# The modulation's lane sums: from TensorE and ScalarE to GpSimd and DRAM

## The reference

```python
silu_c, silu_cc = jax.nn.silu(c), jax.nn.silu(c_ctx)           # 2048 numbers each
mod  = silu_c  @ w_mod[l] + b_mod[l]                           # w_mod[l]: 2048 x 6144
shift, scale, gate = jnp.split(mod[:, None, :], 3, axis=-1)
cmod = silu_cc @ w_mod[l] + b_mod[l]
cshift, cscale, cgate = jnp.split(cmod, 3)
h  = rmsnorm(x,  norm_g[l]) * (1.0 + scale)  + shift           # l = 0, 1
hc = rmsnorm(cx, norm_g[l]) * (1.0 + cscale) + cshift
...
x = x + gate * (y @ w_o[l])
```

## Time and profile before

| | us |
|---|---|
| median of three runs | 2954.16 |
| lowest, highest | 2953.43, 2954.73 |
| profiled execution: span, first to last instruction | 2953.0 |
| its own time outside the span | none is given; the median lies 1.2 above the span |

### The profile page before, as it was taken

One profiled execution on the slowest core, in us unless ns is written; L12 is line 12 of the kernel. 1 busy time (PEld: TensorE's weight loads), 2 busy tenths in 40 slices (PEclk: granted clock), 3 DMA queues, 4 the chain that ended last, 5 costly groups with the idle time before them and its releaser, 6 DMA issues.

```text
span 2953.0 us, 37150 instructions
## 1 busy us (share of the span) xinstructions
PE 2917.4 (99%) x14067; PEld 2392.3 (81%) x14067; DVE 1942.1 (66%) x2730; ACT 1266.1 (43%) x2044; POOL 216.7 (7%) x303
## 2 busy tenths in 40 slices
PE   9999999999999999999999999999999999999998
PEld 7897788888888888888888887777888888878877
DVE  6886466668868888888865834445545645666655
ACT  5443355553444344443555223333333324435444
POOL 1000000011001001010100000000000100102000
PEclk9999999999999999999999999999999999999999
DMA  8987956568767878878764743333343653766444
GB/s 281 297 299 266 314 175 193 151 201 283 254 211 266 279 259 277 271 263 279 266 205 140 230 137 122 117 111 129 106 139 130 228 185 90 258 228 208 136 137 156
DMA packets 313557, 611.05 MB, mean 207 GB/s; under 512 B 29303, under 2 KB 90452, under 8 KB 312484
## 3 DMA queue, kind: packets, MB, share of 16 engines
q1 hardware_dynamic: 294236, 544.74, 57.0%
q0 software_dynamic: 18176, 62.61, 5.9%
q10 hardware_dynamic: 968, 1.33, 0.1%
HBM read 567.93 MB, written 41.84 MB: 206 GB/s over the span
## 4 chain that ended last, share of the span: by engine, by line
PE 94%; DVE 3%; ACT 1%; issue 1%; DMA 0%; POOL 0%; SPq 0%; POOLq 0%; ACTq 0%; DVEq 0%
PE acc L679 28%; PE acc L681 27%; PE acc L680 27%; PE acc L1491 3%; PE acc L1465 2%; PE acc L1479 2%; DVE w_lo L496 1%; PE acc L1042 1%; PE acc L1463 1%; ACT w_hi L490 1%; PE acc L1440 1%; PE acc L756 0%; PE acc L609 0%; PE acc L705 0%; DVE at_st L1654 0%
## 5 line engine op out<-in xcount | busy, mean ns | idle before, releaser
L679 PE MATMUL acc<-w_hi,a_hi 128*128 128x512 f32 (+3 forms) x3736 | 1482.8, 397 | 8.6 <-DVE w_lo L496 6.5
L681 PE MATMUL acc<-w_hi,a_lo 128*128 128x512 f32 (+3 forms) x3736 | 1447.8, 388 | 0.0
L680 PE MATMUL acc<-w_lo,a_hi 128*128 128x512 f32 (+3 forms) x3736 | 1445.0, 387 | 0.0
L496 DVE TENSOR_TENSOR w_lo<-raw,w_hi 128x1024 fp32r<-128x1024 f32 (+3 forms) x778 | 932.2, 1211 | 342.1 <-ACT w_hi L490 337.2
L490 ACT ACTIVATE w_hi<-raw 128x1024 fp32r<-128x1024 f32 (+3 forms) x778 | 805.4, 1047 | 723.2 <-PE acc L681 671.4
L679 PEld LDWEIGHTS acc<-w_hi,a_hi 128*128 128x128 f32 x3736 | 702.6, 188 | 165.5 <-issue 18.7
L681 PEld LDWEIGHTS acc<-w_hi,a_lo 128*128 128x128 f32 x3736 | 701.7, 188 | 142.8
L680 PEld LDWEIGHTS acc<-w_lo,a_hi 128*128 128x128 f32 x3736 | 703.3, 188 | 126.5
L533 DVE SCALAR_TENSOR_TENSOR lanes_b<-raw,ct,lanes_b 128x1024 f32<-128x1024 f32 x150 | 189.5, 1305 | 0.0
L533 DVE SCALAR_TENSOR_TENSOR lanes_c<-raw,ct,lanes_c 128x1024 f32<-128x1024 f32 x120 | 157.6, 1357 | 0.0
L1537 ACT ACTIVATE pb<-acc,at_st 128x256 f32<-128x256 f32 (+4 forms) x144 | 71.1, 494 | 137.7 <-DVE at_st L1652 90.2
(11 more groups left out here) (422 smaller groups left out, 1772.9 us busy)
## 6 DMA issues: line engine op xcount, KB each, us to landing
raw<-in_w_mod SPq DMA_DIRECT2D x192, 512.0 KB, 4.8
raw<-in_w_in SPq DMA_DIRECT2D x128, 512.0 KB, 5.1
raw<-in_w_mlp_in SPq DMA_DIRECT2D x128, 512.0 KB, 4.3
raw<-in_w_mlp_out SPq DMA_DIRECT2D x128, 512.0 KB, 5.4
raw<-in_e_w_in SPq DMA_DIRECT2D x104, 512.0 KB, 4.0
raw<-in_w_o SPq DMA_DIRECT2D x64, 512.0 KB, 5.6
raw<-in_o_w_in SPq DMA_DIRECT2D x64, 512.0 KB, 4.6
raw<-in_w_in SPq DMA_DIRECT2D x56, 448.0 KB, 5.0
```

The costliest lines, as they stand in the source:

```text
L496: nc.vector.tensor_tensor(w_lo[:, n % SPLITS, 0:size], raw[:, r % RAWS, 0:size], w_hi[:, n % SPLITS, 0:size].bitcast(F32), ALU.subtract)\
L679: nc.tensor.matmul(o, s.lhs(0, kt, tt), wh, start=kt == 0 and not s.goes_on, stop=False)
L680: nc.tensor.matmul(o, s.lhs(0, kt, tt), wl, start=False, stop=False)
L681: last = nc.tensor.matmul(o, s.lhs(1, kt, tt), wh, start=False, stop=end)
```

## The change

The four functions go. In their place stands one on GpSimd, `lanes_reduce`, tied to nine steps of the walk. It waits for the piece's adds, adds each of the lanes' four quarters (128 x 512) over the partitions in place (the sum then stands in every partition), waits for that, and takes partition 0 as the row of 2 x 1024. In pieces 4 and 5 it halves the row and stores its two halves to MODF. Then it stores the row to a new DRAM tensor MODR, waits until it has landed, loads it back into `mc` with 128 numbers down the partitions and eight columns per vector, element by element, waits again, and counts `lanes_out` up itself. The hook of a step runs behind that step's stores or squares.

```diff
@@ -24,6 +24,7 @@
 P = 128
 DM = 2048
 KT = DM // P
+NPIECE = 10
 SEQ = 256
 CTX = 256
 HD = 128
@@ -217,6 +218,7 @@
         CMPK = dram("CMPK", (HD, 2 * NCMP))
         CMPV = dram("CMPV", (2 * NCMP, HD))
         MODF = dram("MODF", (2, 2, DM))
+        MODR = dram("MODR", (NPIECE, 2, CH))
         U2 = dram("U2", (CTX + SEQ, 6656))
         O2 = dram("O2", (CTX + SEQ, DM))
         U3 = dram("U3", (CTX + SEQ, 4416))
@@ -445,7 +447,8 @@
         ct_ready, bias_in, bias_zero = sem("ct_ready"), sem("bias_in"), sem("bias_zero")
         vec_ctx, vec_x = sem("vec_ctx"), sem("vec_x")
         lanes_done, lanes_out = sem("lanes_done"), sem("lanes_out")
-        sums_done, sums_kept, sums_turned = sem("sums_done"), sem("sums_kept"), sem("sums_turned")
+        lanes_reduced, row_halved, row_out, row_back = (sem("lanes_reduced"), sem("row_halved"), sem("row_out"),
+                                                        sem("row_back"))
         WIDE = tuple(range(NQ - 1))
 
 
@@ -599,43 +602,28 @@
             if upto == 2 * CH // P:
                 last.then_inc(lanes_done, 1)
 
-        def lanes_sum(pe, j):
-
-            pe.wait_ge(vec_ctx, KT * (j + 1))
-            pe.wait_ge(vec_x, KT * (j + 1))
-            if j:
-                pe.wait_ge(lanes_out, j)
+        def lanes_reduce(pool, j):
+
+            pool.wait_ge(vec_ctx, KT * (j + 1))
+            pool.wait_ge(vec_x, KT * (j + 1))
             for q in range(4):
-                last = nc.tensor.matmul(acc[32 * q:32 * q + 32, 4, :], ones[:, 0:32],
-                                        lanes_of(j)[:, q // 2, q % 2 * G:(q % 2 + 1) * G], start=True, stop=True)
-            last.then_inc(sums_done, 1)
-
-        def sums_keep(act, j):
-
-            act.wait_ge(sums_done, WIDE.index(j) + 1)
-            gate = j in (4, 5)
-            nc.scalar.activation(lanes_of(j)[:, 0, 0:G], acc[:, 4, :], ACT.Copy, scale=0.5 if gate else 1.0)\
-              .then_inc(sums_kept, 1)
-            if gate:
-                act.wait_ge(sums_kept, WIDE.index(j) + 1)
+                t = lanes_of(j)[:, q // 2, q % 2 * G:(q % 2 + 1) * G]
+                nc.gpsimd.partition_all_reduce(t, t, P, bass.bass_isa.ReduceOp.add).then_inc(lanes_reduced, 1)
+            pool.wait_ge(lanes_reduced, 4 * (j + 1))
+            row = lanes_of(j)[0:1, :, :]
+            if j in (4, 5):
+                nc.gpsimd.tensor_scalar(row, row, 0.5, None, ALU.mult).then_inc(row_halved, 1)
+                pool.wait_ge(row_halved, j - 3)
                 for v in range(2):
-                    act.dma_start(MODF[0, v, (j - 4) * CH:(j - 3) * CH].rearrange("(h n) -> h n", h=2),
-                                  lanes_of(j)[64 * v:64 * v + 64:32, 0, 0:G]).then_inc(rows_put, 16)
-
-        def sums_turn(pe, j):
-
-            pe.wait_ge(sums_kept, WIDE.index(j) + 1)
-            for i in range(4):
-                last = nc.tensor.transpose(acc[:, 4, i * P:(i + 1) * P], lanes_of(j)[:, 0, i * P:(i + 1) * P], ident[:, :])
-            last.then_inc(sums_turned, 1)
-
-        def sums_out(act, j):
-
-            act.wait_ge(sums_turned, WIDE.index(j) + 1)
+                    pool.dma_start(MODF[0, v:v + 1, (j - 4) * CH:(j - 3) * CH], lanes_of(j)[0:1, v, :]).then_inc(rows_put, 16)
+            pool.dma_start(MODR[j:j + 1, :, :], row).then_inc(row_out, 16)
+            pool.wait_ge(row_out, 16 * (j + 1))
             layer, c = (0, 8 * j) if j < 6 else (1, 8 * (j - 6))
-            nc.scalar.activation(mc[:, layer, :, c:c + 8].rearrange("p v (h i) -> p v h i", h=2),
-                                 acc[:, 4, :].rearrange("p (i v h x) -> p v h i x", i=4, v=2, h=2)[:, :, :, :, 0], ACT.Copy)\
-              .then_inc(lanes_out, 1)
+            for v in range(2):
+                pool.dma_start(mc[:, layer, v, c:c + 8], MODR[j, v, :].rearrange("(n p) -> p n", p=P),
+                               allow_slow_non_contiguous=True).then_inc(row_back, 16)
+            pool.wait_ge(row_back, 32 * (j + 1))
+            pool.sem_inc(lanes_out, 1)
 
         def lanes_keep(act, j):
             act.wait_ge(lanes_done, 1)
@@ -647,10 +635,9 @@
         beside = {}
         for j, ((name, i, c), (name2, i2, c2)) in enumerate(zip(sum_spots, keep_spots)):
             if j in WIDE:
-                places, at, _ = sum_wide[j]
-                for n, engine, f in ((0, "pe", lanes_sum), (5, "act", sums_keep), (6, "pe", sums_turn), (11, "act", sums_out)):
-                    name, i, c = places[at + n]
-                    stages[name].hook(engine, i, c, lambda eng, f=f, j=j: f(eng, j))
+                name, i = (("qkv", 5), ("gates_a", 0), ("mlp", 1), ("mlp", 5), ("mlp", 11), ("mlp", 14), ("mlp", 19),
+                           ("mlp", 22), ("mlp", 27))[j]
+                stages[name].hook("pool", i, 0, lambda pool, j=j: lanes_reduce(pool, j))
                 continue
             places, at, wide = sum_wide[j]
             for m in range(wide):
```

## The result

| | before | after |
|---|---|---|
| median us (4 runs each, same chip) | 2954.44 | 2986.36 |
| lowest, highest | 2953.43, 2955.94 | 2981.26, 2987.61 |
| span of the profiled execution | 2953.0 | 2985.8 |
| granted clock of TensorE, mean | 0.999 | 0.994 |

After is slower: ratio 1.0105, 95% interval 1.0091 to 1.0120, 31.9 us. I had forecast +104 us.

The account below looks back on a forecast made before the run. TensorE, busy 99% of the span, was taken to bound the kernel. Losses of 116.5 us at GpSimd's places less 12.9 us saved gave +103.6 us, a span of 3056.6 and a median of 3058 us; range 2941 to 3600 us.

Parts of the forecast that it names:

- piece 2: Reduction ahead of MLP step 2's squares, which TensorE transposes: window 27.2 us, needed 65.6, lost 38.4.
- piece 8: Reduction ahead of the mid_gain and sub_row loads, for which VectorE waits: window 19.0 us, needed 60.6, lost 41.6.
- R: One GpSimd all-reduce over 128x512, four per piece: taken as eight passes, 11.4 us; bounds 1.15 to 103 us.
- the windows: At each of nine places, how long GpSimd may be away before TensorE stands; losses there summed to 116.5 us.
- rival 1: All hidden: R near a single pass and no load, so every window is wide enough; 2941 us, chance 0.13.
- contention, at nothing: Slowing of VectorE's adds beside GpSimd's all-reduces, put at 0 us in the forecast.
- The bound that I worked out for it: VectorE's adds slowed throughout a reduction: about 12 us for each of seven pieces, up to +84 us.
- The saving: Lane sum (0.99 us) and turning (0.44 us) gone from TensorE, nine times: 12.9 us.
- The load: GpSimd loading code at each change of kind, 14 times, 5 us each.
- The DRAM trip: The row to DRAM and back into columns, issued by GpSimd: 10 us per piece, between 5.5 and 13.3.
- The halving: Pieces 4 and 5 also halve the row on GpSimd, 2048 columns on one partition: about 1.9 us.
- Pieces 0, 1 and 4: Waits for the clearing of cmp_v, for q and behind the bias row: lost 3.4, 6.2 and 19.5 us.

Follow-up runs that it names:

- e5: The changed kernel without its 36 all-reduces; partition 0's partial sums still go through DRAM: 2941.02 us, ratio 0.9955 to the kernel before.
- e4: The changed kernel with each of the 36 all-reduces covering one column of its 128x512 tile: 2946.02 us, ratio 0.9964 to the kernel before.
- e3: The changed kernel with both moves, that of e1 and that of e2, together: 2962.51 us, ratio 1.0027 to the kernel before.
- e6: The kernel before plus three groups of 12 all-reduces (maximum, 128x512) on GpSimd in the MLP, where nobody waits for them: 2964.03 us, ratio 1.0030.
- e1: The changed kernel with piece 2's reduction moved to step 3 of the stage before the MLP: 2972.31 us, ratio 1.0059 to the kernel before.
- e2: The changed kernel with the loads of mid_gain and sub_row put ahead of piece 8's reduction: 2973.86 us, ratio 1.0068 to the kernel before.
- e8: The kernel before with its lane sums kept on TensorE, but the turning replaced by the row through DRAM on ScalarE's queue: 2951.04 us, ratio 0.9986.

## Why the prediction was wrong

**The balance, from the runs.** Off TensorE: 2941.02 - 2954.44 = -13.4 (e5). The loads: +5.0 (e4 over e5). The two narrow places: +23.9 (after over e3). The rest of the all-reduces' time, beside VectorE: +16.5 (e3 over e4). Sum +31.9, as measured. The last two terms are not sharp: e4 keeps the narrow places, so what they cost with hardly any all-reduce is in its 5.0. Against e5 the rest is 21.5 us, loads included. e6 bears the last term out from outside: 9.3 us for 71.3 us of all-reduces, so 16 us for the 123.7 us in after, or 25 us if it goes by what VectorE lost (21.4 us there, 57.5 in e3). The traces say the same by place. Against e5, matmul by matmul, after falls behind by 17.3 us at piece 2, by 9.6 at piece 8, and by 21.1 at the other seven, 48.0 in all.

**The step that failed first: R.** "Eight passes", 11.4 us, a count of halvings priced with a square. Measured: 3.4 us, inside my bounds and near their lower end. Everything that I lost at the windows was made of 4R = 45.6 where 13.7 was true. By the formula of my own rival 1 (the places lose 8R - 11.2) R = 3.44 gives +3 us, 2957 us. With the measured load and DRAM trip put in as well, the same windows give a loss of 14.1 us at piece 2 and 14.4 at piece 8, near the 14.1 and 12.5 that were measured: the windows hold, R didn't. The rival had the right condition; I should have seen that the forecast hung on a number for which no row spoke, and that its two ends gave opposite signs.

**The step that failed second: "contention, at nothing".** The row was before me: VectorE's adds at 4.04 us beside a square. I dismissed it because an all-reduce "touches memory far more thinly". The trace says that a split or add beside it isn't done before it is, 3.3 us in place of 1.2. e6 shows the same with no other change, and operations with a PSUM input stay clean. The bound that I worked out for it would have missed it too: with 4R = 13.8, VectorE's 12.0 us of work become 19.6 by the ratio 4.04 / 2.47 (which makes the prediction's 39.7 us 65, not 64), less 1.8 us of idle and 5.6 of cushion, that is nothing. The size of VectorE's part holds, though not as an even slowing: (1999.6 - 1942.1) / 9 = 6.4 us more per piece in e3, where the bound has 7.6. The cushion doesn't. Of 6.4 us, 1.8 to 2.4 reached the end (16.5 to 21.5 us over nine pieces), and in e6 3.1 of 7.1 a group: idle and buffers together take some 4 us, not 7.4.

**Point by point.** The saving: 12.9 predicted, 13.4 measured, right. The load: 5 us predicted, at a change of kind only, right in kind and in number; 6.0 to 9.3 measured. The DRAM trip: 10 us predicted, 13.6 measured (933.82 to where the columns have landed, about 947.4), and without effect by itself. The halving: 1.9 us predicted, 5.80 and 8.78 measured on one partition. Piece 2: needed 42.6 us (912.48 to 955.07) and not 65.6, still over the 27.2 of the window; lost 14.1 (e1) where I had 38.4. Piece 8: lost 12.5 (e2) where I had 41.6; VectorE stood for `sub_row`, the second of the two rows that I had put behind the reduction. Pieces 3, 5 and 6 "nothing", piece 7 7.4: against e5, pieces 3, 6 and 7 cost 1.6, 2.6 and 1.2 us. Pieces 0, 1 and 4: the waits that I had named (for the clearing of `cmp_v`, for q, for the bias row) did not appear at all, and piece 1 costs nothing. What piece 0 and pieces 4 and 5 do cost against e5, 7.3 and 8.4 us, goes with short waits for `w_lo`, that is VectorE. And a stall's price was taken as its length; the clock adds to it, 11.4 us of TensorE's busy time in after.

**Right in direction, by two causes of which I had one.** The deciding places, 23.9 us, outweigh the saving of 13.4 on their own; the contention that I left out, 16.5 to 21.5, does so too, and is what stays when the places are mended. The direction was in part luck: with the true R and all else as I had it, my sum gives 2957 us, within the 6 us that I called no change. That the kernel came out clearly slower lies in loads and a DRAM trip longer than I had taken them, and in the contention.

## What to carry to other kernels

Work that moves to an idle GpSimd is paid on VectorE where VectorE reads two SBUF tiles: before counting the gain, look for VectorE rows beside GpSimd's, take a pair apart, and count, as here, one held VectorE operation for each GpSimd instruction. When a forecast rests on an operation that no row shows, and its bounds give both signs, price both ends with all their side effects, not the middle of one estimate. An undo of each half (e5, e8) tells in two runs which half pays: here the row through DRAM paid, and the sums on GpSimd did not.

## What the hardware showed beyond that

- A sum over 128 partitions of a 128x512 tile takes 3.4 us on GpSimd, a maximum 2.0 us (after, e6); with one column the sum takes 0.46 us in the median (e4).
- The return to ordinary code costs 7.7 to 8.2 us of idle (1180.51 and 1231.11 in after), the way to the all-reduce 6.0 to 6.3 at pieces 2, 4, 6 and 8, but 8.3 and 9.3 at pieces 0 and 5. Why these two are longer no run shows.
- A multiplication of 1x2048 on GpSimd takes 5.80 to 8.78 us, and VectorE's pair of adds beside the first took 5.87 us in place of 2.47.
- After an idle of 10.7 us that ended at 957.15, TensorE's matmuls take 0.63 us in place of 0.39 until about 961.5, with the granted clock at 0.53 in the mean (after).
- The holding goes both ways: where a VectorE operation with two SBUF inputs has begun just before, the all-reduce takes up to 4.9 us in place of 3.3 (918.75 in after, the longest of the 36).
